# A two-layer decoder step on one core: value pages move from GpSimd's DMA queue to SyncE's, the scaling of the weights moves to ScalarE, and the order of the mixing loop is rearranged

## The chip, the core and the metric

The kernel runs on one core of a Trainium2 chip. The metric is the device time in microseconds (us) of the whole program. TensorE (PE) does the matmuls and transposes, VectorE (DVE) and ScalarE (ACT) the elementwise work, GpSimd (POOL) a little elementwise work and some DMAs, and SyncE (SP) issues nearly all DMAs.

## What is computed

One inference step of a trunk of two layers. 256 prompt tokens and 64 new tokens (8 sequences of 8) go through it together, so most matmuls have 320 columns. Each layer is a SwiGLU feed-forward, a token mix, and a second feed-forward:

```python
def trunk(x, sample):
    for l in range(DEPTH):                                   # DEPTH = 2
        x = x + 0.5 * _swiglu(_rmsnorm(x, ...), ...)
        past = (paged(cache_moba_k[l]), paged(cache_moba_v[l]), paged(cache_fox_k[l]),
                paged(cache_fox_v[l]), paged(cache_fox_logf[l]), state_hgrn[l])   # sample only
        o, rows = _token_mix(_rmsnorm(x, norm_mix_g[l]), ..., past)
        x = x + o
        x = x + 0.5 * _swiglu(_rmsnorm(x, ...), ...)

def _token_mix(h, ...):       # three groups of heads on one projection of h
    oa = _moba_attend(...)    # 6 heads: attention over the best 3 of 4 past blocks of 256 keys, and the new ones
    of = _fox_attend(...)     # 5 heads: attention with forget gates
    oc, s_new = _hgrn2_recurrence(...)   # 5 heads: a gated linear recurrence
    return concat(oa, of, oc) @ w_out
```

Each of the 8 sequences has 1,024 past keys and values in 8 pages of 128 rows. The pages lie scattered in HBM, and a page table says which page is which. The page of one layer has 384 columns for the first group (moba) and 320 for the second (fox), all in float32.

## The kernel before

Weights stream through two buffers, `raw[0]` and `raw[1]`. ScalarE makes the high part (`hi`, L623), VectorE the low part (`lo`, L896), and TensorE multiplies (`dense`, L1503). This is the feed-forward and the projections, most of the time.

The token mix of each layer is a loop over `BLOCKS` = 32 blocks: i = 4 q + n, where q is the sequence (0 to 7) and n the block of two pages (0 to 3). Every engine has its own copy of this loop, with its own order of work, and semaphores tie them together. On TensorE block i has:

- `turn_keys(i + 1)`: 12 transposes of the key pages of the next block (L1662). It waits for the pages (`k_in`) and for the past sums that GpSimd writes beside them (`past_in`).
- `block_scores(i)`: 16 matmul records at L1686. In the text T(q,n) is the time at which this group ends in block n of sequence q.
- for n = 1 `turn_weights(q-1)` (L1697), for n = 2 `values(q-1)` (L1713 to L1721), which multiplies with the eight value pages of the sequence before and counts `values_used` up page by page, and for n = 3 `turn_outputs(q-1)` (L1729).
- for the first blocks the prompt's attention, head by head: `prompt_scores` (L1741, L1744), `turn_probs` (L1753), `prompt_out` (L1766).
- from block `LEVEL0` = 14 to 22 the recurrence's `products` (L1809), then its end keys, own sums, state sums and squares (blocks 23 to 27).

PSUM banks 0 to 2 form a ring; each new user waits until the one before was copied out by ScalarE or VectorE.

SyncE loads the keys: `key_page(q, pg)` waits until the page that held this slot was transposed (there are four slots, so two blocks), reads the page's number (L488), and issues two DMAs (L489, L490). GpSimd has three jobs in one queue: `add_past` (L574), a small copy for each block; `load_values(q)` at block (q,2), which waits for `values_used` page by page, reads the number and issues two DMAs (L581, L582); and `scale_weights(q-1)` at block (q,0), or at the end for q = 7, which multiplies the softmax weights by the block factors (L594, L596).

After the loop TensorE has `turn_weights(7)`, `values(7)`, `turn_outputs(7)`. Then the output projection starts: it waits for `raw[0]` with `w_out`, which SyncE loads after its last key page and after the DMAs of the recurrence's states (L522, L524).

## Time and profile before

| | |
|---|---|
| median of 3 runs | 1854.87 us (1849.67 to 1855.2) |
| the profiled execution | 1848.9 us |
| its span, first to last instruction | 1847.2 us |
| mean granted TensorE clock | 0.950 |
| TensorE busy with matmuls | 1679.9 us, 91% |
| VectorE, ScalarE, GpSimd busy | 1090.3, 641.4, 225.2 us |
| loop of the token mix, layer 0 (block 0's scores to block 30's) | 408.9 to 629.0 us |
| the same in layer 1 | 1309.8 to 1528.3 us |
| first matmul of the output projection | 661.69 us and 1559.06 us |

The page's busy shares are means over stages. In the mixing loop TensorE is less busy and its clock is lower than in the feed-forward, and the change touches only this loop and its end. A time in a table of stretches counts from the span's start.

### The profile page before, as it was taken

What the parts mean: (1) busy time and instruction counts of PE and PEld (TensorE: products, weight loads), DVE (VectorE), ACT (ScalarE), POOL (GpSimd) and SP (SyncE); (2) the same over time, 40 slices, a digit from 0 to 9 for tenths busy, and PEclk for the clock granted to TensorE, in tenths of its full rate; (3) what the DMA queues carried; (4) which work ended last, traced back from release to release, by engine and by line L of the source; (5) the groups of instructions that cost most, each with busy time, mean ns of one, the idle gap of its engine ahead of it and who ended that gap; (6) DMA issues with size and microseconds to landing.
All of it is one profiled execution on the core that took longest, in us unless ns stands there. A gap on an engine that the chain in (4) does not pass through costs nothing. (4 is left out here: it accounts for less than half of the span.)

```text
span 1847.2 us, 35981 instructions
## 1 busy us (share of the span) xinstructions
PE 1679.9 (91%) x13569; PEld 1552.4 (84%) x13569; DVE 1090.3 (59%) x1817; ACT 641.4 (35%) x880; POOL 225.2 (12%) x407
## 2 busy tenths in 40 slices
PE   5999999977988679999999999998798885999997
PEld 5999999955666479999999999997566664899996
DVE  7666555456566556665566655544655663766645
ACT  3333332334433324333343333323433342433322
POOL 0000000022445400000000000001135352000000
PEclk9999999989988889999999999998897997999998
DMA  6444455464556635444454544655456573544443
GB/s 185 141 155 147 134 161 140 124 182 147 184 167 213 204 99 160 158 138 147 148 160 139 156 140 145 157 151 144 147 168 211 168 223 118 158 157 145 145 148 114
DMA packets 284178, 287.45 MB, mean 156 GB/s; under 512 B 26542, under 2 KB 272998, under 8 KB 283942
## 3 DMA queue, kind: packets, MB, share of 16 engines
q1 hardware_dynamic: 268290, 239.52, 42.7%
q0 software_dynamic: 14464, 46.48, 7.9%
q8 instruction: 64, 1.05, 0.2%
q10 hardware_dynamic: 1316, 0.03, 0.1%
q14 instruction: 44, 0.36, 0.1%
HBM read 279.58 MB, written 6.40 MB: 155 GB/s over the span
## 5 line engine op out<-in xcount | busy, mean ns | idle before, releaser
L1503 PE MATMUL PS<-xh,whi 128*128 128x320 f32 x1920 | 597.3, 311 | 13.9 <-DMA K<-in_consts 10.8
L1503 PE MATMUL PS<-xh,wlo 128*128 128x320 f32 x1920 | 594.7, 310 | 0.0
L1503 PE MATMUL PS<-xl,whi 128*128 128x320 f32 x1920 | 594.5, 310 | 0.0
L896 DVE TENSOR_TENSOR wlo<-raw,whi 128x2048 fp32r<-128x2048 f32 (+2 forms) x185 | 406.8, 2199 | 263.4 <-ACT whi L623 260.5
L623 ACT ACTIVATE whi<-raw 128x2048 fp32r<-128x2048 f32 (+2 forms) x185 | 340.6, 1841 | 609.3 <-PE PS L1503 601.7
L1503 PEld LDWEIGHTS PS<-xh,whi 128*128 128x128 f32 x1920 | 361.7, 188 | 15.9 <-issue 11.1
L1503 PEld LDWEIGHTS PS<-xh,wlo 128*128 128x128 f32 x1920 | 361.7, 188 | 0.7 <-issue 0.2
L1503 PEld LDWEIGHTS PS<-xl,whi 128*128 128x128 f32 x1920 | 361.7, 188 | 0.0
L1503 PE MATMUL PS<-hh,whi 128*128 128x320 f32 x704 | 217.5, 309 | 0.0
L1503 PE MATMUL PS<-hh,wlo 128*128 128x320 f32 x704 | 217.5, 309 | 0.0
L1503 PE MATMUL PS<-hl,whi 128*128 128x320 f32 x704 | 217.5, 309 | 0.0
L574 POOL COPY key_pages<-past 128x10 f32<-128x10 f32 x64 | 14.7, 238 | 1179.2 <-DVEq L891 999.6
L735 ACT ACTIVATE keys_t<-PS 128x512 f32<-128x512 f32 x128 | 76.2, 598 | 200.4 <-PE PS L1662 200.2
L1662 PE MATMUL PS<-K,key_pages 128*128 128x128 f32 x768 | 124.5, 323 | 10.2 <-DMA key_pages<-in_cache_fox_k 3.3
L1503 PEld LDWEIGHTS PS<-hh,whi 128*128 128x128 f32 x704 | 132.1, 188 | 0.0
L1503 PEld LDWEIGHTS PS<-hh,wlo 128*128 128x128 f32 x704 | 132.1, 188 | 0.0
L1503 PEld LDWEIGHTS PS<-hl,whi 128*128 128x128 f32 x704 | 132.1, 188 | 0.0
L1662 PEld LDWEIGHTS PS<-K,key_pages 128*128 128x128 f32 x768 | 105.4, 167 | 24.1 <-issue 16.8
L1125 DVE COPY keys_t<-PS 128x512 f32<-128x512 f32 x64 | 44.3, 692 | 120.2 <-PE PS L1662 119.8
L933 DVE TENSOR_TENSOR tmp<-PS,rstd 128x320 f32<-128x320 f32 x88 | 42.6, 488 | 88.1 <-PE PS L1503 87.9
L581 POOL DMA_DIRECT2D value_pages<-in_cache_moba_v x128 | 69.6, 544 | 114.5 <-issue 73.2
L641 ACT ACTIVATE tmp<-tmp 128x320 f32<-128x320 f32 x88 | 40.3, 463 | 116.0 <-DVE tmp L933 116.0
(252 smaller groups left out, 1862.5 us busy)
## 6 DMA issues: line engine op xcount, KB each, us to landing
raw<-in_ffn_w_gate SPq DMA_DIRECT2D x45, 1024.0 KB
raw<-in_ffn_w_up SPq DMA_DIRECT2D x45, 1024.0 KB
raw<-in_ffn_w_down SPq DMA_DIRECT2D x32, 1024.0 KB
raw<-in_w_in SPq DMA_DIRECT2D x64, 512.0 KB
key_pages<-in_cache_moba_k SPq DMA_DIRECT2D x128, 192.0 KB, 2.5
value_pages<-in_cache_moba_v POOLq DMA_DIRECT2D x128, 192.0 KB, 2.9
key_pages<-in_cache_fox_k SPq DMA_DIRECT2D x128, 160.0 KB, 3.0
value_pages<-in_cache_fox_v POOLq DMA_DIRECT2D x128, 160.0 KB, 3.5
```

The source lines that it names most:

```text
L574: pool.tensor_copy(key_pages[:, pg:pg + 2, AW + BW:AW + BW + BH], past_of[:, L, q, 2 * n:2 * n + 2, :]).then_inc(past_in, 1)
L581: pool.dma_start(value_pages[:, pg, 0:AW], vmv[:, ds(page + L * NPOOL, 1), :].rearrange("p a c -> p (a c)")).then_inc(v_in[pg], 16)
L623: act.activation(whi[s][:, 0:nk, :], raw[s][:, 0:nk, :], ACT.Copy).then_inc(hi_done[s], 1)
L641: act.activation(tmp[j][:, :], tmp[j][:, :], ACT.Silu).then_inc(silu_done, 1)
L735: act.activation(keys_t[i % 2][:, 4 * u:4 * u + 4, :], PS[:, bank, :].rearrange("p (j c) -> p j c", j=4), ACT.Copy).then_inc(read_act[bank ...
L896: dve.tensor_tensor(wlo[s][:, 0:nk, :], raw[s][:, 0:nk, :], whi[s][:, 0:nk, :].bitcast(F32), ALU.subtract).then_inc(split_done[s], 1)
L933: dve.tensor_tensor(tmp[j][:, :], PS[:, j, 0:NT], rstd[:, :], ALU.mult).then_inc(gate_scaled, 1)
L1125: dve.tensor_copy(keys_t[i % 2][:, 4 * u:4 * u + 4, :], PS[:, bank, :].rearrange("p (j c) -> p j c", j=4)).then_inc(read_dve[bank], 1)
L1503: last = te.matmul(out, w[wslot][r, kt, cols], x[r, at, :], start=start and n == 0 and m == 0, stop=stop and n == len(ktiles) - 1 and m == 2)
L1662: last = te.transpose(PS[:, bank, 128 * j:128 * j + 128], key_pages[:, pg % 4, 128 * pr:128 * pr + 128], ident)
```

## The change

- The value pages are loaded by SyncE. Sequence 0's eight pages come before the loop. For the others, four pages (a half) come at block (q,2) and four at (q,3), each half behind the two key pages of that turn of SyncE's loop.
- ScalarE scales the weights, as five activations right behind the factors.
- GpSimd keeps only `add_past` and gets the clearing of `a_blocks`, which VectorE did.
- `turn_probs` and `prompt_out` come one block later on TensorE; the levels of the recurrence start at block 15; VectorE masks the prompt scores (`prompt_mask`) and takes the levels' products (`take`) earlier in its block, and its factors are made a block ahead of their use; `copy_probs` comes last in ScalarE's block; `prompt_out_lo` comes after the loop.

```diff
-LEVEL0 = 14
+LEVEL0 = 15
...
+                def load_values(q, half):
+
+                    for pg in range(4 * half, 4 * half + 4):
+                        sp.wait_ge(values_used, (L * DB + q) * NPG + pg + 1)
+                        page = sp.value_load(pages[0:1, q * NPG + pg:q * NPG + pg + 1], min_val=0, max_val=NPOOL - 1)
+                        sp.dma_start(value_pages[:, pg, 0:AW], vmv[:, ds(page + L * NPOOL, 1), :].rearrange("p a c -> p (a c)")).then_inc(v_in[pg], 16)
+                        sp.dma_start(value_pages[:, pg, AW:AW + BW], vfv[:, ds(page + L * NPOOL, 1), :].rearrange("p a c -> p (a c)")).then_inc(v_in[pg], 16)
...
+                sp.wait_ge(win_used, L * 32 + 36)
+                settle(sp)
+                for half in range(2):
+                    load_values(0, half)
...
-                for q in range(DB):
-                    for pg in range(4 if q == 0 else 0, NPG):
-                        key_page(q, pg)
+                for i in range(BLOCKS):
+                    q, n = divmod(i, NBLK)
+                    if i + 2 < BLOCKS:
+                        for pg in range(2):
+                            key_page((i + 2) // NBLK, 2 * ((i + 2) % NBLK) + pg)
+                    if n >= 2 and q >= 1:
+                        load_values(q, n - 2)
...
-                load_values(0)
+                pool.memset(a_blocks[:, :, :], 0.0).then_inc(products_cleared, 1)
                 add_past(2)
                 for i in range(BLOCKS):
                     q, n = divmod(i, NBLK)
                     if i + 3 < BLOCKS:
                         add_past(i + 3)
-                    if n == 0 and q >= 1:
-                        scale_weights(q - 1)
-                    if n == 2 and q >= 1:
-                        load_values(q)
-                scale_weights(DB - 1)
...
                     act.activation(factors[:, :], masked_max[:, :], ACT.Exp, bias=row_stats[:, 0:1]).then_inc(factors_ready, 1)
...
+                    for n in range(NBLK):
+                        act.activation(scaled[n], weight_rows[:, 256 * n:256 * n + 256], ACT.Copy, scale=factors[:, n:n + 1]).then_inc(weights_scaled, 1)
+                    act.activation(new_scaled, new_row_all[:, q, :], ACT.Copy, scale=factors[:, NBLK:NBLK + 1]).then_inc(weights_scaled, 1)
...
                         block_stats(i - 1)
+                    if 1 <= i <= NH:
+                        prompt_mask(i - 1)
                     if n == 0 and q >= 1:
                         gates(q - 1)
+                    if i == LEVEL0 + 1:
+                        take_samples()
+                        take_diagonal()
+                    if LEVEL0 + 2 <= i <= LEVEL0 + 8:
+                        take(i - LEVEL0 - 1)
...
-                    if 2 <= i <= NH + 1:
-                        turn_probs(i - 2)
                     if 3 <= i <= NH + 2:
-                        prompt_out(i - 3)
+                        turn_probs(i - 3)
+                    if 4 <= i <= NH + 3:
+                        prompt_out(i - 4)
```

On SyncE, inside the loop of a layer, two key pages follow each other before the change. A page is one read of its number and two DMAs (the rows called ISA compute the address).

```order
L488 TENSOR_LOAD pages [waits keys_turned]
L488 ISA x2
L489 ISA
L489 DMA key_pages<-in_cache_moba_k 128x384
L490 ISA
L490 DMA key_pages<-in_cache_fox_k 128x320
```

At block (1,2) the changed kernel's SyncE has the last of four value pages and behind it the key page that TensorE needs next.

```order
L487 TENSOR_LOAD pages [waits values_used]
L487 ISA x2
L488 ISA
L488 DMA value_pages<-in_cache_moba_v 128x384
L489 ISA
L489 DMA value_pages<-in_cache_fox_v 128x320
L500 TENSOR_LOAD pages [waits keys_turned]
L500 ISA x2
L501 ISA
L501 DMA key_pages<-in_cache_moba_k 128x384
L502 ISA
L502 DMA key_pages<-in_cache_fox_k 128x320
```

So key pages now stand behind value pages in one queue, and a value page waits for `values_used`. The other place is the end of the loop on SyncE. Before, the states' DMAs and `w_out` follow the last key page:

```order
L490 DMA key_pages<-in_cache_fox_k 128x320
L522 DMA out_hgrn_state_prompt<-tmp 128x64 [waits sample_states_done,prompt_state_copied]
L524 DMA out_hgrn_state_sample<-states 128x8x64
L522 DMA out_hgrn_state_prompt<-tmp 128x64
L524 DMA out_hgrn_state_sample<-states 128x8x64
L522 DMA out_hgrn_state_prompt<-tmp 64x64
L524 DMA out_hgrn_state_sample<-states 64x8x64
L429 DMA raw<-in_w_out 128x5x256 [waits split_done0,keys_turned]
```

With the change they follow the last of sequence 7's eight value pages:

```order
L489 DMA value_pages<-in_cache_fox_v 128x320
L542 DMA out_hgrn_state_prompt<-tmp 128x64 [waits sample_states_done,prompt_state_copied]
L544 DMA out_hgrn_state_sample<-states 128x8x64
L542 DMA out_hgrn_state_prompt<-tmp 128x64
L544 DMA out_hgrn_state_sample<-states 128x8x64
L542 DMA out_hgrn_state_prompt<-tmp 64x64
L544 DMA out_hgrn_state_sample<-states 64x8x64
L430 DMA raw<-in_w_out 128x5x256 [waits split_done0,keys_turned]
```

The load of `w_out` has moved behind eight pages that cannot start before `values(6)` runs.

## Rows read from the trace of the kernel before

**Rows 1.** TensorE's waits in the loop of layer 0, 405 to 629 us: total, times, longest.

```profile
PE PS L1809 <- DVEq L891: 8.5, 6, 2.3
PE PS L1741 <- DVE idle L1239: 7.3, 6, 2.0
PE PS L1753 <- ACT idle L787: 5.4, 5, 1.9
```

**Rows 2.** Stretches in both layers: blocks 3 to 6; T(7,2) to the projection.

```profile
core 0: us, PE busy (x) PEld busy (x) DVE busy (x) ACT busy (x) POOL busy (x), PEclk, DMA share, GB/s
419.80:449.20 29.40, 22.02 (x169) 14.90 (x172) 19.09 (x56) 12.61 (x41) 5.73 (x9) 0.88 0.32 100
629.00:661.70 32.70, 11.49 (x283) 9.41 (x274) 10.68 (x30) 6.61 (x14) 12.69 (x21) 0.74 0.39 121
...
1317.40:1346.70 29.30, 22.04 (x173) 14.90 (x172) 19.14 (x56) 13.06 (x43) 5.88 (x9) 0.88 0.34 102
1528.30:1559.10 30.80, 12.19 (x282) 10.07 (x274) 10.70 (x30) 5.73 (x10) 12.68 (x21) 0.71 0.38 124
```

**Rows 3.** The end of layer 0's loop, in order of time.

```profile
632.03 1.06 PE L1686 MATMUL PS<-keys_t,qz 128*32 128x256 f32 x16
...
646.65 3.62 POOL L594 TENSOR_SCALAR tokp<-weight_rows,factors 112x256 f32<-112x256 f32 x4
648.62 0.98 PE L1697 MATMUL PS<-K,tokp 112*128 112x112 f32 x4 [15.18 <-POOL tokp L594]
...
661.69 0.48 PE L1503 MATMUL PS<-oh,whi 128*128 128x320 f32 x1 [3.60 <-DVE ol L1469]
```

**Rows 4.** SyncE issuing key pages back to back, in order of time.

```profile
618.52 0.33 SPq L489 DMA_DIRECT2D key_pages<-in_cache_moba_k  x1
619.04 0.33 SPq L490 DMA_DIRECT2D key_pages<-in_cache_fox_k  x1
620.14 0.33 SPq L489 DMA_DIRECT2D key_pages<-in_cache_moba_k  x1
```

**Rows 5.** The first value page's matmuls in block (4,2), in order of time.

```profile
546.13 0.39 PE L1713 MATMUL PS<-value_pages,weight_cols 128*16 128x128 f32 x8
```

**Rows 6.** The DMAs of L490, from issue to landing.

```profile
DMA to landing us min/median/max: 2.2/3.0/5.8
```

**Rows 7.** Stretches T(q,2) to T(q+1,1), layer 0: that of q = 6, and the sum of six.

```profile
604.90:623.30 18.40, 15.32 (x228) 9.80 (x220) 9.14 (x27) 11.09 (x23) 10.69 (x20) 1.00 0.83 261
sum 135.10, PE 117.83 PEld 84.81 DVE 80.33 ACT 53.67 POOL 78.77; mean PE 19.64 PEld 14.13 DVE 13.39 ACT 8.95 POOL 13.13
```

**Rows 8.** The same six stretches in layer 1: their sum.

```profile
sum 138.30, PE 118.38 PEld 84.82 DVE 81.11 ACT 53.81 POOL 77.98; mean PE 19.73 PEld 14.14 DVE 13.52 ACT 8.97 POOL 13.00
```

**Rows 9.** Stretches T(q+1,1) to T(q+1,2): sums of six, layer 0 and layer 1.

```profile
sum 44.70, PE 39.59 PEld 31.21 DVE 29.61 ACT 16.77 POOL 4.46; mean PE 6.60 PEld 5.20 DVE 4.93 ACT 2.79 POOL 0.74
...
sum 43.30, PE 38.54 PEld 30.27 DVE 28.85 ACT 17.41 POOL 4.22; mean PE 6.42 PEld 5.04 DVE 4.81 ACT 2.90 POOL 0.70
```

**Rows 10.** A wait of 2 us on TensorE, and the two stretches behind it.

```profile
460.48 0.79 PE L1741 MATMUL PS<-P 64*128 64x128 f32 x2 [2.04 <-DVE idle L1239]
...
460.50:463.90 3.40, 3.40 (x8) 1.96 (x8) 3.10 (x15) 1.36 (x5) 2.06 (x5) 0.50 0.97 344
463.90:467.30 3.40, 3.40 (x12) 2.04 (x12) 0.13 (x1) 0.00 (x0) 0.43 (x2) 0.50 0.44 146
```

**Rows 11.** SyncE's first and last DMA of the six of the states, layer 0.

```profile
621.17 0.37 SPq L522 DMA_DIRECT2D out_hgrn_state_prompt<-tmp  x1
...
626.48 0.66 SPq L524 DMA_DIRECT2D out_hgrn_state_sample<-states  x1
```

**Rows 12.** High and low part of `w_out`'s first chunk, in order of time.

```profile
650.07 1.26 ACT L623 ACTIVATE whi<-raw 128x1280 fp32r<-128x1280 f32 x1
...
659.11 1.49 DVE L896 TENSOR_TENSOR wlo<-raw,whi 128x1280 fp32r<-128x1280 f32 x1 [0.17 <-DVE P L1208]
```

**Rows 13.** The exponentials of 112 x 256 on ScalarE (L746), 405 to 629 us.

```profile
L746 ACT ACTIVATE weight_rows<-PS,minus_max x30: 467/469/478, 416.8 to 628.5; 112x256 f32<-112x256 f32 x30
```

More of the change, by code:

```diff
@@ L574, in add_past @@
                     pool.tensor_copy(key_pages[:, pg:pg + 2, AW + BW:AW + BW + BH], past_of[:, L, q, 2 * n:2 * n + 2, :]).then_inc(past_in, 1)
-                def load_values(q):
-                    for pg in range(NPG):
-                        pool.wait_ge(values_used, (L * DB + q) * NPG + pg + 1)
-                        page = pool.value_load(pages[0:1, q * NPG + pg:q * NPG + pg + 1], min_val=0, max_val=NPOOL - 1)
-                        pool.dma_start(value_pages[:, pg, 0:AW], vmv[:, ds(page + L * NPOOL, 1), :].rearrange("p a c -> p (a c)")).then_inc(v_in[pg], 16)
-                        pool.dma_start(value_pages[:, pg, AW:AW + BW], vfv[:, ds(page + L * NPOOL, 1), :].rearrange("p a c -> p (a c)")).then_inc(v_in[pg], 16)
-                def scale_weights(q):
-                    Q = L * DB + q
-                    if q == 0:
-                        pool.wait_ge(out_tok, (L + 1) * 160)
-                    pool.wait_ge(factors_ready, Q + 1)
-                    pool.wait_ge(weights_ready, (Q + 1) * NBLK)
-                    if Q:
-                        pool.wait_ge(weights_turned, 3 * Q)
-                    for n in range(NBLK):
-                        pool.tensor_scalar(scaled[n], weight_rows[:, 256 * n:256 * n + 256], factors[:, n:n + 1], None, ALU.mult).then_inc(weights_scaled, 1)
-                    pool.wait_ge(new_weights_ready, Q + 1)
-                    pool.tensor_scalar(new_scaled, new_row_all[:, q, :], factors[:, NBLK:NBLK + 1], None, ALU.mult).then_inc(weights_scaled, 1)
                 pool.wait_ge(win_used, L * 32 + 36)
@@ L1227, in rec_inputs @@
                     elif h == 7:
-                        ch.mark(dve.memset(a_blocks[:, :, :], 0.0))
                         ch.mark(dve.memset(a_samples[:, :, :], 0.0))
@@ L1231, in rec_inputs, with prompt_mask @@
                         give(rec_qk_ready)
-                def prompt_max(h):
-                    c = probs[h % 4]
+                def prompt_mask(h):
                     dve.wait_ge(prompt_scores_ready, L * NH + h + 1)
@@ L1427, in _ @@
                         copy_keys(i + 1, 1)
+                    if i in (6, 8, 10, 12, 14, 15):
+                        copy_prompt_out((6, 8, 10, 12, 14, 15).index(i))
+                    if 1 <= i <= NH:
+                        prompt_max(i - 1)
                     if n == 1 and q >= 1:
                         norms(q - 1)
+                    if 2 <= i <= NH + 1:
+                        prompt_norm(i - 2)
                     if 2 <= i <= 7:
                         rec_inputs(i)
-                    if 2 <= i <= NH + 1:
-                        prompt_norm(i - 2)
-                    if 1 <= i <= NH:
-                        prompt_max(i - 1)
-                    if i in (5, 7, 9, 11, 13, 14):
-                        copy_prompt_out((5, 7, 9, 11, 13, 14).index(i))
-                    if LEVEL0 + 1 <= i <= LEVEL0 + 8:
-                        if i == LEVEL0 + 1:
-                            take_diagonal()
-                        else:
-                            take(i - LEVEL0 - 1)
-                        level_factors(i - LEVEL0 - 1)
-                    if LEVEL0 <= i <= LEVEL0 + LEVELS:
-                        level_logs(i - LEVEL0)
+                    if LEVEL0 <= i <= LEVEL0 + 7:
+                        level_factors(i - LEVEL0)
+                    if LEVEL0 - 1 <= i <= LEVEL0 + LEVELS - 1:
+                        level_logs(i - LEVEL0 + 1)
+                    if i == END0 - 2:
+                        end_logs()
                     if i == END0 - 1:
-                        end_logs()
-                    if i == END0:
                         end_keys()
```

37 lines of the change are left out of this document (23 added, 14 removed).

## The prediction, made before the changed kernel ran

> **What bounds the kernel now.** I read the page first, then the waits in the loop, then the stretches, and last the end of the loop in order of time. Outside the mixing loops TensorE works without a break, and the change does not touch it there. In the loop TensorE's long waits are for VectorE and ScalarE: for a level's products, for the masked prompt scores, for the prompt's probabilities, together 21.2 us in layer 0 [rows 1]. A stretch of the loop whose blocks hold prompt attention shows what such waits cost: in 29.4 us TensorE is busy 22.0 us at a clock of 0.88, VectorE 19.1 us [rows 2]. The largest single wait stands at the loop's end: the last scores end at 633.09 us, and TensorE waits 15.18 us until GpSimd, which must first issue the eight value pages of sequence 7, has scaled the weights [rows 3]. From T(7,2) to the projection it is 32.7 us, and 30.8 us in layer 1, with 11.5 and 12.2 us of work [rows 2]. SyncE is never late in the loop, apart from its first blocks.
>
> **The change part by part.** Times are per layer, layer 0 / layer 1, against the profiled execution (1848.9 us, which is 0.3% under the median of the runs, 1854.87).
>
> 1. The scaling moves to ScalarE. Nearest row: an exponential of the same 112 x 256 takes 0.469 us [rows 13]. So 4 x 0.47 and a smaller one of at most 0.47, about 2.3 us a sequence, 18 us a layer, in a ScalarE that works 54 of 135 us in the six stretches [rows 7]. The weights are wanted a block later, so I cost it at nothing in the loop. If this cover were gone it would be 2.3 us a sequence. For sequence 7 the weights are then ready near T(7,2) + 9 instead of + 21.3 (the end of [rows 3]'s scaling less 629.0), and what is late next is the value pages.
>
> 2. The prompt's jobs and VectorE's order, blocks 3 to 6. `prompt_mask` now comes right after the statistics, and `turn_probs` has a block more. The two waits go. The stretch cannot be shorter than VectorE's work, 19.1 us less a clearing of `a_blocks` that lies mostly behind it, so the gain is between the waits' share (4 us) and 10.3 us. I take 22 us for 29.4: -7.0 / -7.0.
>
> 3. SyncE's queue. Two key pages are issued 1.62 us apart, and the second DMA of a page 0.52 us after the first [rows 4]. The key pages of a sequence took 13 us of some 30; with the value pages it is 16 x 1.62 = 25.9 us. What counts is the order. After T(q,2) TensorE frees the first value page in about 0.35 us (0.39 us for its first matmuls [rows 5]), and SyncE issues: four value pages, the keys of block (q+1,1), four value pages, the keys of (q+1,2). The first DMA goes out near T + 1.2 (0.4 and the 0.8 us that lie between two pages' DMAs). Eleven pages later, 17.8 us, comes the page that `turn_keys` of block (q+1,2) wants second; its second DMA is 0.5 us behind and lands after 2.2 to 5.8 us, median 3.0 [rows 6]. With the software queue gone I take 2.4, near the lowest. That is T + 21.9. Then TensorE has half a block's transposes, 0.8, and the scores, 1.06 [rows 3]: **T(q+1,1) cannot be before T(q,2) + 23.8 us**. Before, the six stretches took 135.1 us in all, the shortest 18.4, and 138.3 in layer 1 [rows 7, 8]. TensorE's own work in them is 19.6 us on average, part of it at half clock, so nearly all of them will end at the floor: 6 x 23.8 = 142.8. That is +7.7 / +4.5. With a landing of 3.0 it would be 3.6 us more, and with 5.8 a further 16.8.
>
> 4. The blocks between, T(q+1,1) to T(q+1,2). SyncE's next pages follow directly, so only the waits for the levels' products go. 44.7 and 43.3 us fall to about TensorE's busy time, 39.6 and 38.5 [rows 9], and I leave it there: -5.1 / -4.8. `take` now stands ahead of `scale_outputs` and `copy_outputs` on VectorE, and TensorE's ring waits for these two; two waits of 0.7 us: +1.5 / +1.5.
>
> 5. The clock. At the floor TensorE waits for key pages in one piece: 23.8 less the work of a stretch, 4 to 6 us, in five of six stretches (that of q = 1 holds the most prompt work and waits least). After a wait of 2.04 us, less than half of that, the granted clock was 0.50, 1.2 GHz, for 6.8 us, in which TensorE was busy all the time [rows 10]. At full clock that work is at least 3.4 us, so the price of such a wait is 0 to 3.4 us on top of it; since not everything there goes with the clock I take 2.5. Five times: +12.5 / +12.5.
>
> 6. The end. T(7,2) + 0.45 starts eight value pages on SyncE, 12.9 us. Behind them stand the states' DMAs, 621.17 to 627.14, 6.0 us [rows 11]. Before, these and `w_out` had been hidden under the loop. So `w_out` goes out near T + 19 and lands near + 23. Its high part takes 1.26 us, its low part 1.49 [rows 12], and with the sample's own part the projection starts near T + 26.8. The attention path would be ready at about + 21 (last page landed + 16, then some 5 us of outputs, copies and their high and low parts). 32.7 and 30.8 fall to 26.8: -5.9 / -4.0. If the states' DMAs take 3 us more, the gain shrinks by as much.
>
> 7. `a_blocks` cleared by GpSimd: nothing waits for it before block 16. Past sums: GpSimd is free, and TensorE's late waits for it vanish. Value pages of sequence 0 on SyncE, 13 us: SyncE waits there anyway for the rows' outputs. Nothing for any of these; without that cover, 13 us once a layer.
>
> The sum: -7.0 + 7.7 - 5.1 + 1.5 + 12.5 - 5.9 = +3.7, and -7.0 + 4.5 - 4.8 + 1.5 + 12.5 - 4.0 = +2.7, together +6.4 us. On the profiled execution that is 1855.3, on the median 1861.3 us.
>
> **A rule to weigh against this.** By [rows 4] SyncE's issue is a resource: 1.62 us for a page that carries 352 KB. The Trainium skill, page "DMA: Bandwidth & Descriptors", section "Issuing engines are not separate DMA queues", says that transfers started by different engines run on the same 16 DMA engines, and that using several saves only the sequencer's time, "which is usually small relative to the DMA itself". By that rule the move would be free, and parts 3 and 5 would drop out; the same page's table of issuing engines even prefers SyncE for plain loads. The row does not agree: 352 KB in 1.62 us is 223 GB/s, and in the stretch of q = 6 the core moved 261 GB/s [rows 7], so issue and transfer are of one size here.
>
> **Rivals.** (a) The waits for keys do not cost the clock, or hardly: then part 5 is 0 and the sum is -18.6, 1836 us. For it: the waits stand at the same place in every cycle, and [rows 7] shows a clock of 1.00 for q = 6 in spite of small waits. Against it: [rows 10]. It turns at 2.5 less 6.4 / 10, a price of 1.9 us a wait: under that the kernel is faster. Chance 0.28. (b) Issue time does not bind: DMAs are ahead, the six stretches fall to TensorE's and VectorE's own work, about 20 us each. Then -7 - 15 - 5 - 5 a layer, -64 us in all, 1791 us. Nothing in [rows 4] supports it. Chance 0.04. (c) Landing is slow as well, since value and key pages and the states share one queue: at 4.5 us instead of 2.4 the floor rises by 2.1, twelve times, +25 us: 1886. For it: the 5.8 of [rows 6]. Against it: that row is from a time with two queues busy. Chance 0.14. (d) My forecast, waits for keys and a lower clock that eat both gains: 0.54.
>
> **How the numbers follow.** Less than 0.3% (5.6 us) either way is about what a measurement of this kernel can't tell from no change. My case by itself holds from 1851 to 1875 us (a clock price of 2 to 3.2, a gain in blocks 3 to 6 of 5 to 9): faster 0.01, same 0.17, slower 0.36. (a) gives 0.24 faster, 0.03 same and 0.01 slower, (b) 0.04 faster, (c) 0.14 slower. That is 0.29 faster, 0.20 same, 0.51 slower. The range reaches over (a) with some room for a larger gain in part 2, and to just short of (c): 1830 to 1884 us.
>
> **What the new profile would show.** If right: TensorE's longest waits in the loop are at `turn_keys` for DMAs of `key_pages`, some 20 us a layer and 3 to 6 us each, where [rows 1] has none that long; T(q,2) to T(q+1,1) never under 23.5 us; clock under 0.85 from block 10 on; SyncE issuing without pause for 19 us after each T(q,2); waits for the prompt scores and products under 3 us a layer; no wait of 15 us at the end, but the projection's start released by `w_out`'s `lo`, 26 to 28 us after T(7,2). It would be wrong if SyncE issued a page in clearly less than 1.6 us, if the clock stayed at 1.00 through the waits, or if ScalarE, now with the scaling ahead of its next key copies, became what TensorE waits for.

## The result, and the profile after

The changed kernel takes 1838.21 us, median of 7 runs (1833.99 to 1845.8), beside 1857.96 us for the kernel before on the same chip: ratio 0.9897, 95% interval 0.9871 to 0.9924. Measured a second time, on another chip, it gave 0.9928 (0.9902 to 0.9953). So the change makes the kernel 0.7 to 1.0% faster, where the forecast had it 0.3% slower at 1861. The time lies inside the forecast's range of 1830 to 1884 us, but the direction is the wrong one.

The first two profiles alone would not have shown it. The profiled execution of before (1848.9 us) was faster than all seven of its runs, that of after (1845.8) the slowest of seven. I profiled both once more: the spans are 1847.2 and 1856.6 us for before, 1844.0 and 1842.0 us for after, 9 us apart on average. The stretches below are from the first profile of each kernel; where the second differs by more than 2 us, the text says so. Outside the stretches from T(0,0) to the projection, one in each layer, the profiles spend 1345 and 1350 us before the change and 1348 and 1349 us after it, so the change shows only in the loops.

Stretches of the changed kernel in layer 0, and then layer 1: blocks 3 to 6 (T(0,2) to T(1,2)); the loop from there to T(7,2), called the middle from here on; T(7,2) to the projection, called the end. T(i) with one number is the end of the scores of block i, so T(6) is T(1,2) and T(30) is T(7,2). Columns as in [rows 2].

```profile
422.30:440.40 18.10, 17.32 (x163) 11.81 (x165) 17.65 (x52) 14.33 (x47) 0.79 (x4) 1.00 0.53 162
440.40:633.10 192.70, 157.56 (x2004) 113.35 (x1999) 106.11 (x287) 81.83 (x212) 6.23 (x22) 0.87 0.58 178
633.10:660.00 26.90, 12.48 (x281) 9.86 (x273) 12.74 (x33) 8.43 (x18) 0.00 (x0) 0.71 0.62 175
1321.20:1338.70 17.50, 17.29 (x166) 11.84 (x165) 17.05 (x50) 14.04 (x45) 0.80 (x4) 1.00 0.53 163
1338.70:1528.80 190.10, 159.92 (x2004) 114.53 (x1999) 106.28 (x287) 81.66 (x211) 5.60 (x22) 0.87 0.59 180
1528.80:1555.80 27.00, 13.62 (x285) 10.79 (x273) 12.79 (x33) 8.60 (x19) 0.00 (x0) 0.62 0.63 175
```

The first lines answer to [rows 2]: 29.4 and 29.3 us have become 18.1 and 17.5, with TensorE busy nearly all the time (17.3 us) at full clock; the end has gone from 32.7 and 30.8 us to 27. For the middle the rows of the kernel before are these:

```profile
449.20:629.00 179.80, 157.42 (x1997) 116.02 (x1992) 109.94 (x291) 70.44 (x182) 83.22 (x148) 0.88 0.63 195
1346.70:1528.30 181.60, 156.92 (x2000) 115.08 (x1992) 109.96 (x291) 71.22 (x185) 82.20 (x148) 0.88 0.62 194
```

So the middle got longer by 12.9 and 8.5 us, at nearly the same clock. Layer 0's twelve stretches show where: six from T(q,2) to T(q+1,1), called the six stretches from here on, and the six blocks between. First the sum of the six stretches, to read against [rows 7], and then that of the blocks between, against [rows 9]:

```profile
sum 157.90, PE 123.12 PEld 86.21 DVE 83.34 ACT 66.38 POOL 5.25; mean PE 20.52 PEld 14.37 DVE 13.89 ACT 11.06 POOL 0.87
```

```profile
sum 34.80, PE 34.44 PEld 27.14 DVE 22.77 ACT 15.45 POOL 0.99; mean PE 5.74 PEld 4.52 DVE 3.79 ACT 2.58 POOL 0.16
```

135.1 us became 157.9 (layer 1: 138.3 to 156.2), 44.7 became 34.8 (43.3 to 33.9). What TensorE waits for in the loop of layer 0 is in the main one thing now, the second DMA of a key page; the three rows of [rows 1] are gone. The two largest waits (total, times, longest):

```profile
PE PS L1668 <- DMA key_pages<-in_cache_fox_k: 31.6, 16, 5.7
PE PS L1668 <- DVE idle L1198: 2.1, 2, 1.2
```

The cause, in order of time on SyncE behind T(3,2) = 503.27: the first value page goes out at 504.37; the last of these rows is the second DMA of the key page that `turn_keys` of block (4,2) wants second, at 525.03.

```profile
518.38 0.33 SPq L488 DMA_DIRECT2D value_pages<-in_cache_moba_v  x1
518.90 0.33 SPq L489 DMA_DIRECT2D value_pages<-in_cache_fox_v  x1
520.00 0.33 SPq L488 DMA_DIRECT2D value_pages<-in_cache_moba_v  x1
520.51 1.27 SPq L489 DMA_DIRECT2D value_pages<-in_cache_fox_v  x1
522.55 0.33 SPq L501 DMA_DIRECT2D key_pages<-in_cache_moba_k  x1
523.10 0.33 SPq L502 DMA_DIRECT2D key_pages<-in_cache_fox_k  x1
524.51 0.34 SPq L501 DMA_DIRECT2D key_pages<-in_cache_moba_k  x1
525.03 0.33 SPq L502 DMA_DIRECT2D key_pages<-in_cache_fox_k  x1
```

A value page takes the 1.62 us of [rows 4] as well, and now and then a DMA takes over 1 us to issue. The key page's second DMA, out at 525.03, landed 2.2 us later, and T(4,1) came at 530.69. e1, e2, e6 and e7 below test that this chain is the cause.

### The profile page after: what moved, and what is told of

Same layout as the page of the kernel before. It is cut to its first block and busy times, and to the rows that moved or that the text cites. A ratio compares the mean times of both kernels' runs of the same rounds, so it can differ in the third digit from the quotient of the medians.

```text
span 1844.0 us, 36001 instructions
## 1 busy us (share of the span) xinstructions
PE 1681.4 (91%) x13569; PEld 1548.6 (84%) x13569; DVE 1085.2 (59%) x1815; ACT 671.3 (36%) x960; POOL 20.9 (1%) x73
## 5 line engine op out<-in xcount | busy, mean ns | idle before, releaser
L1509 PEld LDWEIGHTS PS<-xh,whi 128*128 128x128 f32 x1920 | 362.2, 189 | 15.2 <-issue 10.6
L1668 PEld LDWEIGHTS PS<-K,key_pages 128*128 128x128 f32 x768 | 101.1, 164 | 89.2 <-DMA key_pages<-in_cache_fox_k 67.9
L1692 PE MATMUL PS<-keys_t,qz 128*32 128x256 f32 (+1 forms) x1024 | 80.1, 438 | 0.0
L1056 DVE TENSOR_TENSOR P<-PS,rstd 128x320 f32 (+1 forms) x64 | 31.0, 488 | 79.2 <-PE PS L1509 77.9
```

Source lines behind the costliest of these rows:

```text
L1056: dve.tensor_tensor(P[:, ds(i * (4 * NT) + n * NT, NT)], PS[:, n, 0:NT], rstd[:, :], ALU.mult).then_inc(win_used, 1)
L1509: last = te.matmul(out, w[wslot][r, kt, cols], x[r, at, :], start=start and n == 0 and m == 0, stop=stop and n == len(ktiles) - 1 and m == 2)
L1668: last = te.transpose(PS[:, bank, 128 * j:128 * j + 128], key_pages[:, pg % 4, 128 * pr:128 * pr + 128], ident)
L1692: last = te.matmul(o[g], qz[:, q, 2 * g + m, 0:w], k[:, GROUP_TILES[g][m], :, :], start=m == 0, stop=m == 1)
```

## The experiments

Ratios are to the kernel before on the same chip; times of different experiments may be from different chips, so small differences are read from the ratios. "New order" is all of the change but the scaling and the value pages: the order on TensorE, VectorE and ScalarE, the factors and exponentials of a level made a block ahead, and `a_blocks` cleared by GpSimd. The diffs are excerpts, and the remarks behind # are mine.

**e1: value pages back on GpSimd.** Against the changed kernel.

```diff
-                    if n >= 2 and q >= 1:            # SyncE
-                        load_values(q, n - 2)
+                    if n == 2 and q >= 1:            # GpSimd, all eight pages
+                        load_values(q)
```

> The changed kernel, but GpSimd issues the value pages, all eight together after each T(q,2), as in the kernel before; the scaling stays on ScalarE and the new order stays. Theory A (SyncE's queue is what the change pays: value pages between the key pages make the keys of block (q+1,1) and (q+1,2) late): TensorE's 56 us of waits for DMAs into key_pages fall under 6 us; T(6) to T(30), 193 and 190 us in the changed kernel, falls to 180 or less in each layer; the end from T(7,2) to the projection falls from 26.9 to about 22 to 24 us since the states' DMAs and w_out stand behind nothing; in all 30 to 45 us faster than the changed kernel, 1795 to 1808 us. Theory B (the loop's length is set by VectorE, ScalarE and TensorE's clock, and the waits for keys only stand where another wait would): the same waits go, but the stretches stay within 5 us of 193 and 190 us and the time stays at 1828 to 1838 us.

Measured: 1795.86 us, ratio 0.9677 (0.9657 to 0.9697). The middle of the loop, both layers:

```profile
438.50:608.50 170.00, 152.17 (x2004) 110.31 (x1999) 105.98 (x288) 81.33 (x211) 57.61 (x118) 0.91 0.67 206
1309.70:1483.50 173.80, 154.92 (x2005) 113.20 (x2000) 106.00 (x288) 81.27 (x212) 57.08 (x118) 0.89 0.65 201
```

Theory A holds: 22.7 and 16.3 us less than the changed kernel, the six stretches back at 132.2 and 135.2 us, and TensorE's waits for key pages down from 56.0 to 3.7 us. The ends shrank to 23.8 us in layer 1 but hardly (26.7) in layer 0, where GpSimd's last value page went out 17.4 us behind T(7,2), against 14.8 in layer 1. The move of the value pages to SyncE costs 41 to 47 us by the ratios (0.9897 and 0.9928 against 0.9677), 42 by the medians: without it the change would have gained 3.2% instead of 0.7 to 1.0%.

**e2: the same queue, pages by twos.** Against the changed kernel.

```diff
-                    for pg in range(4 * half, 4 * half + 4):
+                    for pg in range(2 * part, 2 * part + 2):
...
-                    if n >= 2 and q >= 1:
-                        load_values(q, n - 2)
+                    if i >= 6:
+                        load_values(*divmod(i - 2, NBLK))
```

> The changed kernel, still all on SyncE's queue, but with the value pages issued by twos, one pair behind the key pages of each block, instead of four behind the keys at n = 2 and four at n = 3. The number of DMAs and of SyncE's instructions is the same, only their place differs. Theory A (it is the order in the queue, eleven pages ahead of the keys that block (q+1,2) wants, that costs): waits for key_pages fall from 56 us to under 10 us, T(6) to T(30) to 180 us or less, the end from 26.9 to about 21 us because only four value pages are left for after T(7,2); 30 to 45 us faster than the changed kernel, 1795 to 1808 us. Theory C (it is the amount of issue work on one engine, 25.9 us of some 30 a sequence, that costs, wherever it stands): the waits only move, stretches stay above 185 us, 1825 to 1838 us, with TensorE now waiting for value pages or for keys of other blocks.

Measured: 1804.42 us, ratio 0.9728 (0.9705 to 0.9752). The middle takes 172.0 and 174.3 us, waits for `key_pages` are 12.5 us in all instead of 56.0. SyncE issues as many DMAs as in the changed kernel. So it is mainly the place in the queue that costs, not the load of 26 us of issue in some 30; 0.5% to e1 is left. The expected end of 21 us did not come: it stayed at 26.8 and 27.6. All eight pages of sequence 7 wait for `values(6)`, which runs behind T(7,2), whatever their place in the queue: in layer 0 the last went out 14.2 us behind T(7,2) and `w_out` 18.4, as in the changed kernel.

**e3: only the scaling, on ScalarE.** Against the kernel before.

```diff
-                    if n == 0 and q >= 1:            # GpSimd
-                        scale_weights(q - 1)
+                    for n in range(NBLK):            # ScalarE, behind the factors
+                        act.activation(scaled[n], weight_rows[:, 256 * n:256 * n + 256], ACT.Copy, scale=factors[:, n:n + 1]).then_inc(weights_scaled, 1)
```

> The kernel before with one part of the change: ScalarE scales the weights, GpSimd still issues the value pages and copies the past sums, the old order of the prompt and level work stays. Theory A (the 15 us wait at the loop's end is the whole effect of this part, ScalarE has room in the loop): the end from T(7,2) to the projection falls from 32.7 and 30.8 to about 22 us, the loop up to T(30) stays within 3 us; 15 to 20 us faster than the kernel before, about 1840 us. Rival (2.3 us of scaling a sequence stand ahead of ScalarE's key copies and exponentials and TensorE waits for them): the loop grows by 1 to 2 us a sequence, 8 to 16 us a layer, and the kernel is no faster than before, 1855 us or more.

Measured: 1853.66 us, ratio 1.0 (0.9984 to 1.0016): neither 1840 nor clearly slower. The ends fell to 26.4 and 23.6 us, 4 and 2 us short of what Theory A expected, but blocks 3 to 6 took 31.8 and 33.3 us and the middle 187.5 and 182.5. The largest wait in layer 0's loop is the third of [rows 1], for the copy of the prompt's probabilities, grown from 5.4 us:

```profile
PE PS L1748 <- ACT idle L782: 9.7, 6, 3.0
```

The loss stands where the probabilities are copied: T(2) to T(14) grew by 9.2 and 8.5 us, while T(14) to T(30) changed by +0.8 and -3.5. So in the old order ScalarE's copy is wanted at once, and the scaling most likely delays it; no run moved only the scaling within ScalarE's block. Both theories were half right. With the new order the same move is worth 0.9% (e1 against e4), all of it at the ends.

**e4: only the new order.** Scaling and value pages as before. The excerpt is against e1.

```diff
+                    if n == 0 and q >= 1:            # GpSimd
+                        scale_weights(q - 1)
```

> The kernel before with the other part alone: the new order of VectorE's, ScalarE's and TensorE's work (mask ahead, probabilities turned a block later, levels one block later, take ahead, products cleared on GpSimd); scaling and value pages stay on GpSimd. Theory A (the order is where the change gains): T(2) to T(6) falls from 29.4 to 18 us and the stretches T(q,1) to T(q,2) by 10 us a layer, the end stays at 31 to 33 us; 25 to 35 us faster than the kernel before, about 1828 us. Rival (the gain of early blocks is taken back later since TensorE's clock falls after any longer run of work, or since VectorE is late elsewhere): T(2) to T(30) shrinks by under 6 us a layer and the kernel is at most 10 us faster, 1848 us.

Measured: 1809.7 us, ratio 0.9763 (0.9739 to 0.9787), a gain of 44 us, above what either theory gave. Blocks 3 to 6 took 18.2 and 18.5 us. The middle:

```profile
439.20:606.60 167.40, 147.88 (x2004) 108.03 (x1999) 106.37 (x287) 70.25 (x181) 86.48 (x148) 0.95 0.68 209
1314.30:1487.20 172.90, 151.33 (x2004) 110.61 (x1999) 106.49 (x288) 70.36 (x183) 86.72 (x148) 0.92 0.65 202
```

Compare TensorE's busy time with the kernel before: 147.9 for 157.4 and 151.3 for 156.9 us, for the same work. It is done at a higher granted clock, 0.95 and 0.92 for 0.88, and the waits ahead of it are fewer. Of the 12.4 and 8.7 us that the middle gains, 9.5 and 5.6 are such busy time.

**e5: VectorE takes the levels' products at the old place.** Against e4.

```diff
-                    if LEVEL0 + 2 <= i <= LEVEL0 + 8:   # ahead of scale_outputs
-                        take(i - LEVEL0 - 1)
+                    if LEVEL0 + 2 <= i <= LEVEL0 + 8:   # behind copy_keys
+                        take(i - LEVEL0 - 1)
```

> The kernel with the new order alone (1809.7 us, value pages and scaling on GpSimd), but VectorE takes the levels' products where the kernel before took them, behind the output scaling, the copy of the outputs and the key copies; the mask ahead, the later turning of the probabilities and the levels one block later stay. Theory A (the order gains in blocks 14 to 26 because a level's products are taken sooner, and with the waits goes the lower clock): T(14) to T(26) grows by 8 to 14 us a layer, TensorE waits again for products about 15 us in all, 1826 to 1838 us. Theory B (the prompt part does it all, by shorter early blocks and a clock that is granted again): blocks 14 to 26 stay within 3 us a layer, 1807 to 1816 us.

Measured: 1812.44 us, ratio 0.9756 (0.9731 to 0.9782), no difference from e4. Blocks 15 to 26 (T(14) to T(26)) took 87.7 and 92.3 us, against 86.3 and 93.5 in e4. Theory A falls: the place of the takes alone is worth nothing that these runs can tell. TensorE waits for the products 2.8 us in all, where the kernel before has 15.9; e5 keeps the factors made a block ahead.

**e6: one more read of the page number per value page.** Against the changed kernel.

```diff
                         page = sp.value_load(pages[0:1, q * NPG + pg:q * NPG + pg + 1], min_val=0, max_val=NPOOL - 1)
+                        page = sp.value_load(pages[0:1, q * NPG + pg:q * NPG + pg + 1], min_val=0, max_val=NPOOL - 1)
```

> The changed kernel with one more read of the page number ahead of each value page on SyncE, which moves no byte. By the rows of the changed kernel such a read with its register operations takes 0.50 us. Theory A (SyncE's issue time is the floor of T(q,2) to T(q+1,1)): each of these twelve stretches grows by 8 x 0.5 = 4 us, from 24.9 to 27.5 us now to 29 to 31.5, part of it taken from the blocks behind; with 4 us at either loop's end 40 to 56 us slower, 1878 to 1894 us. Theory B (the transfers themselves, or TensorE and VectorE, set the stretch): SyncE catches up while the transfers run, under 10 us slower, at most 1848 us.

Measured: 1906.21 us, ratio 1.0268 (1.0247 to 1.029), 63 us over the changed kernel measured beside it (e8). SyncE in this kernel:

```profile
562.84 0.33 SPq L489 DMA_DIRECT2D value_pages<-in_cache_moba_v  x1
563.36 0.33 SPq L490 DMA_DIRECT2D value_pages<-in_cache_fox_v  x1
565.01 0.33 SPq L489 DMA_DIRECT2D value_pages<-in_cache_moba_v  x1
```

A value page takes 2.17 us, 0.55 more. Eight are 4.4 us. The twelve stretches grew from 26.2 us on average (157.9 and 156.2 over 12) to 30.6 (181.0 and 185.8), by 4.4. No byte was added. That is Theory A; the 63 us are 7 above its range of 40 to 56, and the clock of the middle went down too, from 0.87 to 0.82 and 0.80.

**e7: half of the value DMAs on GpSimd.** Against the changed kernel; TensorE waits for both semaphores of a page.

```diff
-                        sp.dma_start(value_pages[:, pg, AW:AW + BW], vfv[...]).then_inc(v_in[pg], 16)
+                        pool.dma_start(value_pages[:, pg, AW:AW + BW], vfv[...]).then_inc(v_fox_in[pg], 16)
```

> The changed kernel with the second DMA of each value page on GpSimd's queue (all eight behind T(q,2), with a semaphore of their own) and the first still on SyncE between the key pages: the same bytes, half of the value DMAs' issue on another engine. Theory A (issue time): SyncE's value page costs 1.1 us instead of 1.62, eight of them 4.2 us less, the floor falls from 26.2 to about 22 us, which is what the stretches take without any value page on SyncE; the ends shrink by 3 to 4 us. 1797 to 1810 us. Theory B (what costs is that value and key pages land in turn, whoever issues them, or that a page comes late if either queue is late): the stretches stay above 25 us, 1825 us or more.

Measured: 1798.77 us, ratio 0.9696 (0.9677 to 0.9715). The six stretches are 136.9 and 137.0 us, 22.8 on average, and the ends 22.9 and 23.5: the last value page landed 14.2 and 14.5 us behind T(7,2), where the changed kernel has 16.7 and 16.6. Theory A.

**e8: the changed kernel again.** No edit.

> The changed kernel once more, for a second profile and a second ratio. Between its first profile and that of the kernel before lie 3.2 us, between the medians 19.7. If the first profile was only one from the slow edge of its runs: median within 1834 to 1842 us again, and the new profile is shorter than 1844 us in the loops, where TensorE's clock differs from run to run, with the same waits for key pages of 50 to 60 us. If instead profiling itself takes the gain: the profile again near 1844 us and the timed runs near 1837.

Measured: 1843.3 us, ratio 0.9928 (0.9902 to 0.9953), a profiled span of 1842.0. The waits for `key_pages` are 51.9 us. The median lies 1 us outside the expected interval; the kernel before has 1856.62 beside it. The stages repeat: 191.6 and 190.2 us in the middle, 27.1 and 27.7 at the ends.

**e9: `w_out` ahead of the states' stores.** Against the changed kernel.

```diff
+                sp.wait_ge(keys_turned, (L + 1) * BLOCKS * 3)
+                wout_chunks(L, 0)
                 sp.wait_ge(prompt_state_copied, L + 1)
```

> The changed kernel with one thing moved on SyncE's queue at the end of each layer's loop: the loads of w_out's first chunk go ahead of the six DMAs that store the recurrent states, still behind the eight value pages. Theory A (the end is set by SyncE's queue: value pages, states, w_out, its high and low parts): the stores' 3.9 us leave the path, the projection starts 23 to 24 us behind T(7,2) instead of 26.9 to 27.7, 6 to 8 us faster than the changed kernel. Theory B (the attention's own path, value pages, outputs, their high and low parts, ends as late): the end stays above 26 us and the time within 2 us of the changed kernel.

Measured: 1835.76 us, ratio 0.9896 (0.9872 to 0.9921). The ends fell to 24.2 and 23.2 us, as Theory A has it, 6.5 us together. The ratio is below both of the changed kernel, but the intervals overlap, so the gain is shown in the stretch and not in the total.

**e10: the mask behind the key copies, in e4.**

```diff
-                    if 1 <= i <= NH:                 # right behind block_stats
-                        prompt_mask(i - 1)
...
                     if 1 <= i <= NH:
+                        prompt_mask(i - 1)
                         prompt_max(i - 1)
```

> The kernel with the new order alone (e4, ratio 0.9763 to the kernel before), but VectorE masks a head's prompt scores where the kernel before did, right ahead of that head's maxima, behind the key copies. Theory A (the early mask gives the 11 us of blocks 3 to 6, and only these): T(2) to T(6) returns from 18 to 26 to 29 us, blocks 7 to 30 stay within 3 us, ratio 0.985 to 0.988. Theory B (removed waits also give back the clock for a long while behind them): the same, and T(6) to T(30) grows from 167 and 173 us towards 180, ratio 0.992 to 1.0. Theory C (it is turning the probabilities a block later that removes the waits, the mask's place does not matter): T(2) to T(6) stays under 20 us, ratio 0.974 to 0.979.

Measured: 1815.87 us, ratio 0.978 (0.975 to 0.9811). T(2) to T(6) took 20.6 and 19.8 us: 2.4 and 1.3 more than in e4. Theory C, nearly: the mask's place ahead of the key copies is a small part. This is not the mask's old place, though. In the kernel before, mask and maxima stand behind `norms`, `rec_inputs` and `prompt_norm` as well; in e10 they stay ahead of these. TensorE waits for masked scores 4.3 us here, none in e4 and 14.4 in the kernel before.

**e11: a version meant to be best.** Against e1, with the last sequence's value pages split between two queues, and `w_out` ahead of the stores.

```diff
-                    for pg in range(NPG):            # GpSimd
+                    for pg in range(4 if q == DB - 1 else NPG):
...
+                for pg in range(4, NPG):             # SyncE, behind the loop's keys, each page with v_last[pg - 4]
+                    sp.wait_ge(values_used, (L * DB + DB - 1) * NPG + pg + 1)
```

> A version meant to beat all so far: value pages on GpSimd and scaling on ScalarE (e1, ratio 0.9677), and at each loop's end the last sequence's eight value pages in two halves, four on GpSimd and four on SyncE with semaphores of their own, then w_out's first chunk, then the states' stores. Theory A (at the end only issue time and landing stand in the way): the last page is issued 7 us behind T(7,2) instead of 14, the projection starts at 17 to 20 us instead of 23.8 to 26.7, 10 to 16 us faster than e1, ratio 0.959 to 0.963. Theory B (w_out's landing and its high and low parts hold it at 22 us or more, or sixteen engines' transfers do): at most 4 us faster than e1, ratio 0.966 or more.

Measured: 1794.75 us, ratio 0.9691 (0.9664 to 0.9717), the same as e1; the ends are 25.5 and 23.7 us. Theory B. In layer 0 T(7,2) is at 610.6, all eight pages are issued by 621.5, and `values(7)` still waits for the fourth of GpSimd's:

```profile
627.85 0.65 PE L1728 MATMUL PS<-value_pages,weight_cols 128*32 128x128 f32 x8 [1.45 <-DMA value_pages<-in_cache_fox_v]
```

This DMA was issued at 620.91 and took 6.9 us to land, the longest of all on its line (L594), min/median/max over the whole run:

```profile
DMA to landing us min/median/max: 2.4/3.7/6.9
```

In e1 the same line has 2.4/3.7/6.1, so only the longest times differ. The 16 DMA engines were 95% busy around it (the last number but one of the first row) and TensorE's clock was 0.52; the second row is layer 1:

```profile
621.00:631.00 10.00, 5.52 (x116) 4.74 (x120) 0.32 (x2) 1.27 (x1) 0.46 (x1) 0.52 0.95 269
1491.00:1500.00 9.00, 5.96 (x126) 5.22 (x126) 0.67 (x3) 1.27 (x1) 0.00 (x0) 0.64 0.89 256
```

In layer 0 the transfers are late, not the issue; `w_out`, issued at 618.8 among them, is likely what they share the engines with, but no run took it away. In layer 1 the pages did come sooner: the last landed 12.9 us behind T(7,2) instead of e1's 18.1, and yet `values(7)` ended at 18.6, as in e1 (18.7), in part because its matmuls ran at the lower clock.

**e12: the kernel before again.** No edit.

> The kernel before, unchanged, for a second profile of it beside those of this call. Its first profiled execution was the fastest of its seven. If that was chance in the granted clock, the second profile has a span of 1850 to 1860 us, the same waits within 2 us, and more time at the lower clock than the first's 187 us; the ratio is 1.00 within its interval.

Measured: ratio 1.0011 (0.999 to 1.0033), a profiled span of 1856.6 us. The waits are the same within 2.5 us, but TensorE's clock was the lower one for 214.6 us instead of 187.3: blocks 3 to 6 of layer 0 took 32.3 us instead of 29.4.

```profile
421.50:453.80 32.30, 24.76 (x169) 16.57 (x172) 19.54 (x58) 12.67 (x41) 6.12 (x9) 0.79 0.31 92
```

The three runs that follow are about the new order: which edit carries its 2.4%?

**e13: probabilities turned at the old block, in e4.** ScalarE's `copy_probs` and VectorE's `copy_prompt_out` go back with it.

```diff
-                    if 3 <= i <= NH + 2:
-                        turn_probs(i - 3)
-                    if 4 <= i <= NH + 3:
-                        prompt_out(i - 4)
+                    if 2 <= i <= NH + 1:
+                        turn_probs(i - 2)
+                    if 3 <= i <= NH + 2:
+                        prompt_out(i - 3)
```

> The kernel with the new order alone (e4, ratio 0.9763), but TensorE turns a head's probabilities two blocks behind its scores and uses them three behind, as the kernel before, with ScalarE's copy and VectorE's copies of the outputs at their old places. Theory A (this one block of slack is what removes the waits of blocks 3 to 14 and, through the granted clock, part of the time behind): T(2) to T(6) goes from 18 to 26 to 30 us and T(6) to T(14) grows too, ratio 0.986 to 0.995. Theory B (the order on VectorE does it, masks and statistics ahead of key copies): T(2) to T(6) stays under 21 us, ratio under 0.981.

Measured: 1811.15 us, ratio 0.9747 (0.9723 to 0.9772), T(2) to T(6) 19.9 us in both layers. The total is that of Theory B. What sets it in e13 is not shown: VectorE's order is one of the edits that it keeps.

**e14: both shifts in the kernel before.** The same lines the other way round, with `LEVEL0 = 15`. VectorE's order stays, but for `copy_prompt_out`, one block later, and `prompt_out_lo`, behind the loop.

> The kernel before with two shifts and nothing else of the order: a head's probabilities are turned and used one block later, and the levels start one block later, which that needs. VectorE's order within a block stays as it was, scaling and value pages stay on GpSimd. Theory A (the slack carries the gain): T(2) to T(6) falls from 29.3 to under 21 us, T(14) to T(18) from 38 to 31 to 33 us, ratio 0.975 to 0.982. Theory B (shifts without VectorE's order gain little, since mask and maxima still come behind the key copies): T(2) to T(6) stays above 25 us, ratio 0.988 or more.

Measured: 1841.51 us, ratio 0.9906 (0.988 to 0.9932). T(2) to T(6) fell only to 24.6 and 25.2 us. Between the two theories, nearer to B. Of TensorE's waits those for the probabilities are gone; those for the levels' products and for the masked scores stay, over both layers, as long as in the kernel before (15.9 and 14.4 us):

```profile
PE PS L1808 <- DVEq L891: 14.9, 10, 2.5
PE PS L1740 <- DVE idle L1239: 14.5, 10, 2.0
```

**e15: the levels one block later, and nothing else, in the kernel before.** `prompt_out_lo` stands behind the loop.

```diff
-LEVEL0 = 14
+LEVEL0 = 15
```

> The kernel before with the levels one block later and nothing else (the low part of the prompt's outputs, which would fall behind the last block, stands behind the loop). Theory A (this shift alone takes the prompt's last jobs and the first level apart and gives the part of the gain that lies in blocks 14 to 18): T(14) to T(18) falls from 38 to under 34 us, T(2) to T(6) stays at 29.3, ratio 0.992 to 0.996. Theory B (it only moves the same waits by a block): T(14) to T(26) stays within 2 us of the 97 us that they take before, ratio 0.998 to 1.002.

Measured: 1846.63 us, ratio 0.9926 (0.99 to 0.9953). T(14) to T(18) fell from 38.2 and 38.8 us to 32.4 and 30.3, so Theory A for the place; T(26) to T(30) gave 4.0 and 2.3 us of it back. The waits for the products stay, at 15.2 us.

## Why the prediction was wrong

By the runs the change is three parts: the new order -44 us (e4), the scaling on ScalarE -14 with it (e1 against e4), the value pages on SyncE +42 (the changed kernel against e1; 41 to 47 by the ratios). The split holds for this order of adding them: without the new order the scaling is worth nothing (e3). By the prediction's own steps:

**Parts 2 and 4, the new order: right in direction, half in size. This is the step that failed.** By stretches, blocks 3 to 6 gave -11.3 and -11.8 us where I took -7.0, and the blocks between gave -9.9 and -9.4 where I took -3.6 and -3.3. Together these two gave -42.4 us over both layers where the sum has -20.9, and the order by itself is -44 (e4). I stopped part 2 at 22 us and part 4 at 39.6 and 38.5, each TensorE's busy time of before. But that busy time was itself stretched by the lower clock: in blocks 3 to 6 it fell from 22.0 to 17.3 us, between from 39.6 to 34.4, in the middle of e4 by 9.5 and 5.6. I charged a clock price to new waits and gave none back for waits removed. The other bound that I named for blocks 3 to 6, VectorE's 19.1 us less a clearing, did not hold either: VectorE was busy 17.65 and 17.05 us in the stretch, with 52 and 50 operations in it instead of 56. The place was wrong too: in e4 the gain stands in the six stretches (123.7 and 124.8 us), none of it between (43.9 and 48.2); in the changed kernel the floor holds the six, and the blocks between come short. The 1.5 us for `take` ahead of the output copies was not there (e5).

Which edit carries the order stays open in part: the levels' shift alone gives 0.7%, with the later probabilities 0.9%, all of it 2.4%. So 1.4% needs what e14 leaves out, and there the long waits for masked scores and products are still whole. Moving the mask behind the key copies, the takes back, or the probabilities back, one at a time in e4, costs 0.2% or nothing. That these cover one another is one explanation, and no run undid two. Another is that the gain lies in edits that e5, e10 and e13 all keep and that no run undid: prompt maxima and mask ahead of `norms` and `rec_inputs`, and a level's factors and exponentials made a block ahead. The waits point to these (2.8 us for products in e5, 4.3 us for masked scores in e10), but this is not tested.

**Part 3, the floor: right, and 2.4 us short.** "T(q+1,1) cannot be before T(q,2) + 23.8 us": the shortest of the twelve was 24.85, the mean 26.2. The page's second DMA went out at T + 20.7 on average (19.8 to 21.8) where I had 19.5, landed 2.4 us later as assumed, and the half block and the scores took 3.1 us instead of 1.9, since they often ran at half clock: in six of the twelve the scores took 1.93 us where [rows 3] has 1.06. e2, e6 and e7 each confirm the mechanism from another side. With it rivals (b), that issue does not bind, and (c), that landing is slow, fall.

**Part 5, the clock: too dear.** I put 2.5 us a wait on top of the floor, +12.5 a layer. TensorE's busy time in the middle is 5.4 and 5.0 us over that of e1, for six such waits 0.9 us each. Parts 3 and 5 together came to +20.2 and +17.0; the six stretches grew by 22.8 and 17.9. The sum was nearly right because one error paid for the other. Rival (a), no clock price and 1836 us, was nearer to this part, but that it met the total, 1838, is luck: it left out a clock price that was there, and took the order at half its size.

**Part 6, the end: right.** 26.9 and 27.0 us for 26.8. From the chain of waits, layer 1, T(7,2) = 1528.8:

```profile
1543.13 0.37 SPq L542
...
1547.11 4.76 DMA raw<-in_w_out
1551.94 1.28 ACT whi L613
1553.24 1.49 DVE wlo L898
1554.74 0.61 DVE ol L1475
```

The states' DMAs took 3.9 us of SyncE, not 6.0, the eight value pages left SyncE 0.9 us later than assumed, and `w_out` took 4.8 us to land, not 4. e9 shows that the states' DMAs were on the path.

**Part 1, the scaling: nothing only in the new order.** e3 shows ScalarE's copy of the probabilities late without it. In layer 0 of the changed kernel TensorE's waits for ScalarE in the loop are 0.4 us in all. In e1 they are larger, 2.8 us for `b` and 3.0 for `weight_cols`, where e4, with the scaling on GpSimd, has 0.6 and 2.4; e1's middle is still 2.6 and 0.9 us longer than e4's. So the scaling may not be quite free there either; the difference is of the size by which two profiles of one kernel differ. **Part 7** held in layer 0; in layer 1, T(0,0) to T(0,2) took 13.7 us instead of 7.6 in one profile and 8.1 in the other. In the first TensorE waits 2.7 us there for a key page (0.7 us in the kernel before) and then works at a clock of 0.55.

**The rule weighed.** By the Trainium skill ("DMA: Bandwidth & Descriptors", "Issuing engines are not separate DMA queues") the move would have been free. e1, e6 and e7 show that it is not here: 0.55 us more of issue a page, with no more bytes, is 63 us. The part of the rule on shared engines has layer 0 of e11 on its side: there two issuers had the last page out 10.4 us behind T(7,2) instead of the changed kernel's 14.2, and it landed at 17.2 instead of 16.7, with the 16 engines 95% busy. It is not so everywhere: in e7 and in layer 1 of e11 two issuers landed the last page 2 to 4 us sooner.

Of the signs that I named, these came: no stretch under 23.5 us (24.7 in the second profile), no waits for prompt scores or products left, the projection 27 us behind T(7,2), released by VectorE's `ol`, which stands right behind the low part of `w_out`. These did not: the waits for keys were 28 us a layer on average, not 20, in more and shorter pieces, and the clock of the middle was 0.87, not under 0.85.

## What to carry to other kernels

When a reordering removes waits, read the busy time behind them at the clock it would have without them: in this kernel TensorE's busy time of before was no lower bound. An in-order DMA queue is a chain like any engine: here the place in it cost more than the load, and cutting the long batch into small pieces behind the loads that are wanted sooner (e2) brought the time within 0.5% of the best. Time a compound change by its parts: here one of three took back 42 of the 58 us that the others gave, and the sum still looked like a small win.

The best version found is e1, 1795.86 us, 3.2% under the kernel before; e7 and e11 lie within 0.2% of it.

## What the runs showed of the hardware

One profile of each kernel can mislead where the difference is 1%: the same program's profiled spans were 1847.2 and 1856.6 us with the same waits within 2.5 us, and with 187 and 215 us at half clock. On SyncE a page, key or value, takes 1.62 us of issue, and one more read of its number with the register operations adds 0.55 (e6); single DMAs take 1.27 or 1.43 us to issue instead of 0.33, which no row explains.
